# The second mixer's block compression with its operands swapped

## The reference, cut to what matters

```python
def phi(t, j):
    blocks = t[:, idx] + cmp_pos[j][None, None, :, None, :]
    flat = swapaxes(blocks, 2, 3).reshape(B, n_cmp, GROUPS, 32 * 64)
    return gelu(flat @ w1[j], approximate=False) @ w2[j]
k_cmp, v_cmp = phi(kc, 0), phi(vc, 1)         # w1[j]: 2048 x 128, w2[j]: 128 x 64
k_cmp = apply_partial_rope(k_cmp, ...)
# "cmp" attention: q . k_cmp, softmax over the 15 blocks, . v_cmp, one of three gated branches
```

## Time and profile before

| | us |
|---|---|
| median of three timed runs | 1687.31 |
| profiled execution, its own time | 1680.67 |
| its span (first to last instruction) | 1678.9 |
| mean granted TensorE clock | 0.952 of full |

### The profile page before, as it was taken

The page is one execution under the profiler, slowest core; times in us unless marked ns, Lnnn a source line. Parts: engine busy times, 40 slices in busy tenths (PEclk is TensorE's granted clock), DMA queues, the critical chain, the costliest instruction groups (busy, mean ns, idle before and its releaser), DMA issues.

```text
span 1678.9 us, 30167 instructions
## 1 busy us (share of the span) xinstructions
PE 1559.0 (93%) x10282; PEld 1427.7 (85%) x10282; DVE 1179.2 (70%) x2190; ACT 816.9 (49%) x1213; POOL 0.2 (0%) x4
## 2 busy tenths in 40 slices
PE   6899886999989999988999799799989999999997
PEld 5788775999879978976999799799978888889996
DVE  4676555788554523756458988899979999986665
ACT  6443555554455334644466566455533334334443
POOL 0000000000000000000000000000000000000000
PEclk9998989999989878979999999899989999999999
DMA  6442332565635411224557576444457777765553
GB/s 253 115 155 90 115 126 86 164 187 178 206 120 174 153 50 51 76 96 155 192 160 225 177 217 197 143 142 140 141 186 241 240 244 237 242 229 187 187 187 125
DMA packets 97772, 276.64 MB, mean 165 GB/s; under 512 B 10788, under 2 KB 37540, under 8 KB 97188
## 3 DMA queue, kind: packets, MB, share of 16 engines
q1 hardware_dynamic: 65808, 240.92, 45.1%
q10 hardware_dynamic: 31892, 34.75, 6.2%
HBM read 259.37 MB, written 16.25 MB: 164 GB/s over the span
## 4 chain that ended last, share of the span: by engine, by line
PE 82%; DVE 9%; ACT 4%; DMA 2%; issue 2%; ACTq 0%; DVEq 0%; SPq 0%; PEldq 0%
PE acc L1058 7%; PE acc L1061 7%; PE acc L1062 7%; PE ring L533 7%; PE ring L536 6%; PE ring L537 6%; PE acc L989 5%; PE acc L993 5%; PE acc L994 5%; PE acc L533 4%; PE ring L1024 3%; PE acc L537 3%; PE acc L536 3%; DVE sb_lo L1512 2%; PE ring L1045 2%
## 5 line engine op out<-in xcount | busy, mean ns | idle before, releaser
L1512 DVE TENSOR_TENSOR sb_lo<-sb_raw,sb_hi 128x1024 fp32r<-128x1024 f32 x450 | 543.8, 1223 | 220.7 <-ACT sb_hi L1120 203.3
L1120 ACT ACTIVATE sb_hi<-sb_raw 128x1024 fp32r<-128x1024 f32 x450 | 469.9, 1057 | 391.3 <-PE acc L1058 168.4
L989 PE MATMUL acc<-sb_XH,sb_hi 128*128 128x256 f32 x800 | 235.6, 295 | 18.5 <-DVE sb_lo L1512 13.3
L533 PE MATMUL ring<-sb_XH,sb_hi 128*128 128x256 f32 x784 | 224.4, 286 | 7.2 <-DVE sb_lo L1512 7.2
L993 PE MATMUL acc<-sb_XL,sb_hi 128*128 128x256 f32 x800 | 227.7, 285 | 0.0
L994 PE MATMUL acc<-sb_XH,sb_lo 128*128 128x256 f32 x800 | 227.5, 284 | 0.0
L537 PE MATMUL ring<-sb_XH,sb_lo 128*128 128x256 f32 x784 | 223.5, 285 | 0.0
L536 PE MATMUL ring<-sb_XL,sb_hi 128*128 128x256 f32 x784 | 223.4, 285 | 0.0
L1058 PE MATMUL acc<-sb_hi,sb_coefh 128*128 128x512 f32 x512 | 200.9, 392 | 7.2 <-DVE sb_coefl L2018 7.2
L1061 PE MATMUL acc<-sb_lo,sb_coefh 128*128 128x512 f32 x512 | 200.5, 392 | 0.0
L1062 PE MATMUL acc<-sb_hi,sb_coefl 128*128 128x512 f32 x512 | 200.1, 391 | 0.0
(11 more groups left out here) (315 smaller groups left out, 2631.6 us busy)
## 6 DMA issues: line engine op xcount, KB each, us to landing
sb_raw<-wstream SPq DMA_DIRECT2D x450, 512.0 KB, 3.6
ahead<-sb_early ACTq DMA_DIRECT2D x100, 128.0 KB, 2.3
sb_area<-ahead ACTq DMA_DIRECT2D x100, 128.0 KB, 3.2
sb_area<-gains ACTq DMA_DIRECT2D x4, 512.0 KB, 4.8
sb_area<-consts SPq DMA_DIRECT2D x1, 1782.0 KB, 16.4
sb_area<-mem ACTq DMA_DIRECT2D x1, 1024.0 KB, 11.5
relvec<-sb_area ACTq DMA_DIRECT2D x1, 1024.0 KB
sb_area<-keys ACTq DMA_DIRECT2D x1, 1024.0 KB, 5.2
```

The costliest lines, as they stand in the source:

```text
L533: ins = mm(out, w[0], x[0], start=first, stop=False)
L989: ins = mm(o, w[0], XH[:, c, :], start=c == 0, stop=False)
L1120: A(hi[:, r, :], raw[:, r, :], ACT.Copy).then_inc(S("hi_ready"), 1)
L1512: tt(lo[:, r, :], raw[:, r, :], hi[:, r, :].bitcast(F32), ALU.subtract).then_inc(S("lo_ready"), 1)
```

## The change

Each weight chunk of `w1[j]` is now the moving operand, with its `hi` and `lo` halves side by side (256 columns in two stretches of 128, taken from one buffer `halves` that holds both), and the 30 block columns are stationary. Each chunk takes two products, one with `kwh` and one with `kwl` stationary, 64 in all; `kwl` x `lo` is thereby computed too. The result of a j is 30 rows of two 128-wide sums (with `hi` and with `lo`), all in one bank (`crow`). ACT copies it to SBUF; four products with a 30 x 30 identity as moving operand turn it, and add the two sums, into the bank `chid` (line "chid" of the new code). `merge_half(0, 0)` stands between `crow` and the turning, `merge_half(0, 1)` between the turning and `ck2`. `crot` and `cv2` with the copies behind them move into step 0 of the attention, after `score`; only `pv` of the `cmp` units waits for `cv2_done`. On DVE the first third of `rope` now comes between `feed(cw1, 0)` and `feed(cw1, 1)`, the other two after them. On ACT both Gelus come after `feed(merge, 0)` and before `merge_copy(0)`.

```diff
@@ -167,6 +167,9 @@
         for i in range(len(units) + 2):
             if i < len(units):
                 job(("score", u0 + i), "att_scaled")
+            if units is ATT3 and i == 0:
+                job(("crot",), "crot_done")
+                job(("cv2",), "cv2_done")
             if u0 == 0 and i < len(MEM):
                 job(MEM[i], "ckv_copied")
             if 1 <= i <= len(units):
@@ -238,11 +241,9 @@
     job(("vv",), "r2_copied")
     for i in range(3):
         job(("rope", i), "roped")
-    for j in range(2):
-        job(("chid", j), "chid_done")
+    job(("crow",), "crow_copied")
+    job(("chid",), "chid_done")
     job(("ck2",), "ck2_done")
-    job(("crot",), "crot_done")
-    job(("cv2",), "cv2_done")
     attention(ATT3, len(ATT1) + len(ATT2))
     for i in range(4):
         job(("ysT", i), "ysT_ready")
@@ -291,8 +292,8 @@
         fixc = sb("fixc", at, 256)
         at += 256
         raw = sb("raw", at, NR * PC).rearrange("p (r n) -> p r n", r=NR)
-        hi = sb("hi", at + NR * PC, NR * PC, F32R).rearrange("p (r n) -> p r n", r=NR)
-        lo = sb("lo", at + 2 * NR * PC, NR * PC, F32R).rearrange("p (r n) -> p r n", r=NR)
+        halves = sb("halves", at + NR * PC, 2 * NR * PC, F32R).rearrange("p (s r n) -> p s r n", s=2, r=NR)
+        hi, lo = halves[:, 0], halves[:, 1]
         at += 3 * NR * PC
 
         XH = sb("XH", at, KC * T, F32R).rearrange("p (c t) -> p c t", c=KC)
@@ -405,6 +406,7 @@
         ofox = pl.take(NT * 512).rearrange("p (t n) -> p t n", t=NT)
         onsa = pl.take(NT * 512).rearrange("p (t n) -> p t n", t=NT)
         ott = pl.take(512)
+        crow = ott[0:2 * NCMP].rearrange("p (j s n) -> p j s n", j=2, s=2)
         mg = pl.take(NT * 2 * DM).rearrange("p (t b n) -> p t b n", t=NT, b=2)
 
         pl = Place(stage)
@@ -710,6 +712,8 @@
             def pv(u):
                 kind, t, heads, n = UNITS[u]
                 b = bank(("pv", u))
+                if kind == "cmp":
+                    pe.wait_ge(S("cv2_done"), 1)
                 pe.wait_ge(S("att_turned"), u + 1)
                 k = min(n, P)
                 nk = n // k
@@ -741,6 +745,8 @@
                         else:
                             (proj_T if MEM[i][0] == "ck" else proj_R)(MEM[i], MEM[i])
                     if units is ATT3:
+                        if i == 0:
+                            compressed_keys()
                         for j, t in merge_halves(i):
                             merge_half(j, t)
                     if 1 <= i <= len(units):
@@ -918,30 +924,42 @@
                 done(ins, ("rope", i))
 
             pe.wait_ge(S("kw_split"), 1)
+            b = bank(("crow",))[0:2 * NCMP].rearrange("p (j s n) -> p j s n", j=2, s=2)
             for j in range(2):
-                b = bank(("chid", j))
-                (q0, r0), (q1, r1_) = piece(("cw1", j), 0), piece(("cw1", j), 1)
-                for lp in range(16):
-                    k = lp % 8
-                    ins = mm3(b[:, 0:2 * NCMP], part(r0 if lp < 8 else r1_, lambda z: z[:, k * P:(k + 1) * P]),
-                              (kwh[:, j, lp, :], kwl[:, j, lp, :]), lp == 0, lp == 15,
-                              q0 if lp == 0 else q1 if lp == 8 else 0)
-                done(ins, ("chid", j))
+                for k in range(2):
+                    q, r = piece(("cw1", j), k)
+                    for i in range(8):
+                        lp = 8 * k + i
+                        rows = halves[:, :, r, i * P:(i + 1) * P]
+                        ins = mm(b[:, j], kwh[:, j, lp, :], rows, start=lp == 0, stop=False)
+                        if i == 0:
+                            ins.then_inc(S("piece_free"), 1)
+                        ins = mm(b[:, j], kwl[:, j, lp, :], rows, start=False, stop=lp == 15)
+            done(ins, ("crow",))
             pe.wait_ge(S("acc_free"), NT * 3)
             merge_half(0, 0)
-            pe.wait_ge(S("chid_done"), 2)
+            pe.wait_ge(S("crow_copied"), 1)
+            b = bank(("chid",))
+            for j in range(2):
+                for s in range(2):
+                    ins = mm(b[:, 32 * j:32 * j + 30], crow[:, j, s], ident[0:30, 0:30], start=s == 0, stop=s == 1)
+            done(ins, ("chid",))
+            merge_half(0, 1)
+            pe.wait_ge(S("chid_done"), 1)
             done(mm(bank(("ck2",))[:, 0:30], C("w2k", 0, 128), chid[:, 0, 0:30], start=True, stop=True), ("ck2",))
-            merge_half(0, 1)
-            pe.wait_ge(S("ck2_done"), 1)
-            done(mm(bank(("crot",))[:, 0:30], K("rot"), ckc[:, 0, 0:30], start=True, stop=True), ("crot",))
-            b = bank(("cv2",))
-            for g in range(2):
-                ins = mm(b[0:NCMP, g * HD:(g + 1) * HD], chid[:, 1, g * NCMP:(g + 1) * NCMP], C("w2v", 0, 64),
-                         start=True, stop=True)
-            done(ins, ("cv2",))
+
+            def compressed_keys():
+
+                pe.wait_ge(S("ck2_done"), 1)
+                done(mm(bank(("crot",))[:, 0:30], K("rot"), ckc[:, 0, 0:30], start=True, stop=True), ("crot",))
+                b = bank(("cv2",))
+                for g in range(2):
+                    ins = mm(b[0:NCMP, g * HD:(g + 1) * HD], chid[:, 1, g * NCMP:(g + 1) * NCMP], C("w2v", 0, 64),
+                             start=True, stop=True)
+                done(ins, ("cv2",))
+
             pe.wait_ge(S("fox_rows"), 1)
             pe.wait_ge(S("r2_copied"), 3)
-            pe.wait_ge(S("cv2_done"), 1)
             attention(ATT3, len(ATT1) + len(ATT2))
             pe.wait_ge(S("att_out"), len(UNITS))
             for i in range(4):
@@ -1163,6 +1181,9 @@
                             ins = A(attP[:, u % 2, k * n:(k + 1) * n], attS[:, u % 2, k * n:(k + 1) * n], ACT.Exp,
                                     bias=amx[:, u % 4, k:k + 1], accum_out=asum[:, u % 4, k:k + 1])
                         link(ins, "att_exp")
+                    if units is ATT3 and i == 0:
+                        link(A(cvr[0:NCMP].rearrange("p g d -> p (g d)"), got(act, ("cv2",))[0:NCMP, 0:P], ACT.Copy),
+                             "cv2_done")
                     if units is ATT1:
                         kind, k = name = MEM[i]
                         feed(name)
@@ -1339,14 +1360,17 @@
                 copy_job(("fv", i), fv[:, :, 256 * i:256 * i + 256], "r2_copied")
             feed(("vv",))
             copy_job(("vv",), vv, "r2_copied")
+            feed(("cw1", 0))
+            feed(("cw1", 1))
+            link(A(crow.rearrange("p j s n -> p (j s n)"), got(act, ("crow",))[0:2 * NCMP], ACT.Copy), "crow_copied")
+            feed(("merge", 0))
+            b = got(act, ("chid",))
             for j in range(2):
-                feed(("cw1", j))
-                b = got(act, ("chid", j))
-                link(A(chid[:, j, 0:30].rearrange("p (g n) -> p n g", g=2), b[:, 0:30].rearrange("p (n g) -> p n g", g=2), ACT.Gelu), "chid_done")
-            feed(("merge", 0))
+                ins = A(chid[:, j, 0:30].rearrange("p (g n) -> p n g", g=2),
+                        b[:, 32 * j:32 * j + 30].rearrange("p (n g) -> p n g", g=2), ACT.Gelu)
+            link(ins, "chid_done")
+            merge_copy(0)
             link(A(ckc[:, 0, 0:30], got(act, ("ck2",))[:, 0:30], ACT.Copy), "ck2_done")
-            link(A(cvr[0:NCMP].rearrange("p g d -> p (g d)"), got(act, ("cv2",))[0:NCMP, 0:P], ACT.Copy), "cv2_done")
-            merge_copy(0)
             attention(ATT3, len(ATT1) + len(ATT2))
             for i in range(4):
                 turned(("ysT", i), 2 * i)
@@ -1549,6 +1573,10 @@
                         else:
                             link(stt(out=o, in0=b, scalar=scale, in1=bias, op0=ALU.mult, op1=ALU.add), "att_scaled")
                         link(V.tensor_reduce(amx[:, u % 4, 0:m], o, AX.X, ALU.max, negate=True), "att_max")
+                    if units is ATT3 and i == 0:
+                        link(tt(ckc[:, 1, 0:30], got(dve, ("crot",))[:, 0:30], K("sinc"), ALU.mult), "crot_done")
+                        link(tt(ckc[:, 2, 0:30], ckc[:, 0, 0:30], K("cosc"), ALU.mult))
+                        link(tt(ckc[:, 2, 0:30], ckc[:, 2, 0:30], ckc[:, 1, 0:30], ALU.add), "cmpk_ready")
                     if units is ATT1:
                         if i < len(MEM):
                             feed(MEM[i])
@@ -1852,18 +1880,21 @@
             feed(("fv", 1))
             feed(("vv",))
             dve.wait_ge(S("ng_ready"), 1)
-            for i in range(3):
+
+            def roped(i):
+
                 b = got(dve, ("rope", i)).rearrange("p (k t) -> p k t", k=2)
                 o = t2[:, 8 + 2 * i:10 + 2 * i, :]
                 r = rt[:, i % 2, :].rearrange("p (k t) -> p k t", k=2)
                 link(tt(r, b, K("sinq").unsqueeze(1).to_broadcast([P, 2, T]), ALU.mult), "roped")
                 link(tt(o, o, K("cosq").unsqueeze(1).to_broadcast([P, 2, T]), ALU.mult))
                 link(tt(o, o, r, ALU.add), "roped_all" if i == 2 else "dve_step")
+
             feed(("cw1", 0))
```

(6 more changed lines are left out.)

## The result

| | before | after |
|---|---|---|
| median on the chip of the first comparison, us | 1687.35 (4 runs) | 1670.51 (4 runs, 1668.36 to 1671.29) |
| ratio, 95% interval | | 0.9896, 0.9878 to 0.9914 |
| profiled execution, us | 1680.67 | 1668.36 |
| its span, us | 1678.9 | 1666.5 |

Faster, as forecast, by 16.8 us between medians against 12.7 forecast, and 12.3 between the two profiled executions. The interval of this first comparison leaves out the forecast (12.7 us is a ratio of 0.9925). Two more comparisons on other chips gave 0.9922 (0.9905 to 0.9939) and 0.9925 (0.9906 to 0.9944), which both hold it: about 13 us by ratio, 15.1 and 13.1 between medians.

What follows compares the result with a forecast made beforehand. PE, busy 93% of the span, was taken as the bound. The stage's 27.5 us becoming 14.2 saves 13.3, less 0.65 coming back: 12.7 us, so 1687.31 becomes 1674.6 us, range 1669.5 to 1683.

Steps and rivals of the forecast that it cites:

- the slow clock belongs to this stage: Compression stage: 30-column products run at 1.2 GHz from 574.60, and `merge_half(0, 0)` pays part of the price.
- Layer: First compression layer on PE: 64 products of 256 moving columns at 0.1135 us each, 7.3 us.
- Turning: Added after `merge_half(0, 0)`: four fp32 products at 0.2 us each, 0.8 us, bounds 0.4 and 1.7.
- Layer to score: From the layer's first product to the first `score`: 14.2 us after the change, 27.5 before.
- The wait for `lo` before the merge half: PE before `merge_half(0, 0)`: waits 0.1 us for DVE's merge 0 pieces, at most 0.5 with the semaphores.
- `crot` and `cv2` coming back: Behind the first `score`: their 0.65 us of work returns there, while the 0.62 us wait for `cv2_done` goes.
- carrying over the 6.6 us: Whole kernel: the timed median stays 6.6 us above the profiled execution, as before the change.
- the 2 + 2 us: Allowances: 2 us each way for where the stage's clock changes, another 2 for slow clock in `score(0)` and the following merge half.
- The clock at 1.2 GHz in the new layer: Rival, chance 0.10: layer takes 13.6 us instead of 7.3, gain 3.4 us, 1683.9 us.
- the two-stretch operand at 0.213: Rival, chance 0.07: new layer's moving operand streams at 0.213 us instead of 0.1135, gain 6.3 us, 1681.0 us.
- the pace of unrounded fp32: Rival, chance 0.04: new layer's products take 0.40 us each, layer 25.6 us, 5.6 us lost, 1692.9 us.
- The given-back case: Rival, chance 0.05: attention gives back part through late chain, late merge pieces or slow clock; gain 9.6 us, 1677.7 us.

Runs made afterwards that it cites:

- DVE's order alone: Kernel before with only the first third of `rope` moved between the two feeds, old products kept: 1684.65 us, ratio 0.9999 against before.
- the swap alone: Kernel before with the new products and the turning, DVE's old order, `crot` and `cv2` ahead of the attention: 1678.94 us, ratio 0.9965.
- the change with the old order: Changed kernel with all `rope` operations on DVE put back ahead of both feeds: 1672.69 us, ratio 0.9930 against before.
- the tail alone: Kernel before with only `crot`, `cv2` and their copies moved into step 0 of the attention: 1681.67 us, ratio 0.9988.
- 32-product version: Changed kernel with `kwh` and `kwl` stationary together, six turning products, all `lo` before `rope`: 1669.78 us, 0.9912; with the change's DVE order, one execution, 1673.44 us.

## Why the prediction was right

*Mechanism.* The step "the slow clock belongs to this stage" carried most of the gain, and held: the clock falls in the old products without any idle (DVE's order alone), and the new ones keep it over a gap (the swap alone). From layer to score the granted clock was 0.67 to 0.72 in all four profiled executions with the old products. Of the ten with the new ones nine had 1.00, and the tenth, the one with 3.37 us of idle PE, 0.90. Which property of the old products does it, the 30 moving columns or the 128 stationary ones loaded for each, no run separates. Of the 12.8 us that the stage lost in the profile, the layer gives 10.4 (18.00 to 7.56), `merge_half(0, 0)` 2.2 (5.17 to 2.97) and the tail that left the stage 1.25; the turning costs 1.0. An estimate of what the clock is worth in it: j = 1 at the pace of j = 0 would have taken 48 x 0.101 = 4.8 us less, and with the 2.2 of the merge half that makes 7.0. The gap is 2.2 of the rest, and the fewer products about 3.4, less 1.0 for the turning.

*Terms.* Layer 7.3 forecast, 7.56 measured: the first step took 0.31 us, and the pace was 0.115 against 0.1135. That the two-stretch operand is the cause of this 0.0015 isn't shown, since the same stream went at 0.1165 until 570.23 and at 0.114 from there on. Merge halves 2.9 and 2.9, measured 2.97 and 2.96. Turning 0.8, measured 1.0. `ck2` 0.2, 0.23. Layer to score 14.2, measured 14.7. The wait for `lo` before the merge half, 0.1, was none. `crot` and `cv2` coming back 0.65, measured 1.0, at a granted clock of 0.57.

*What was off is the median.* 1674.6 was forecast, 1670.51 measured, inside the range. The first comparison had 16.8 us between medians, the later two 15.1 and 13.1. The step at fault is carrying over the 6.6 us by which the timed runs of before stood above its profiled one: for the change that distance was 2.2. The 4 us beyond the forecast gain in the first comparison are no merit of the prediction's mechanism: the profiles have 12.8 us in the stage (27.5 to 14.7), and the rest isn't placed. The attention behind the stage is where the profiled executions differ most. Windows from the first score to the last transpose, of before, of the change with the old order, of the tail alone:

```profile
596.50:730.10 133.60, 131.03 (x807) 114.36 (x808) 64.89 (x138) 62.39 (x176) 0.00 (x0) 0.85 0.20 64
```
```profile
584.00:719.40 135.40, 132.87 (x815) 116.15 (x814) 63.21 (x139) 62.88 (x178) 0.00 (x0) 0.85 0.18 57
```
```profile
596.10:733.30 137.20, 134.67 (x815) 117.11 (x814) 63.33 (x139) 62.91 (x177) 0.00 (x0) 0.83 0.17 55
```

With the two shown above: 133.6 us at 0.85, 137.2 at 0.83, 138.2 at 0.82, 142.7 at 0.79. PE's work is nearly the same in all, so the length follows the granted clock. Before's profiled execution has the shortest of all fourteen profiled; that it stood for a typical one was the error, and the 2 + 2 us allowed for it were few where the attention alone spans 9. The work ahead of the layer and behind the attention, the same in all versions, adds to this: the layer starts between 566.5 and 570.1, and what follows the attention spans 5 us. That before's unprofiled runs have longer attentions fits their times but isn't shown, since they leave no timeline. Whether the old products also make the attention's clock worse on average stays open too: four profiles with them give 133.6 to 142.7, the ten others 135.4 to 138.2.

*Rivals.* The clock at 1.2 GHz in the new layer, the two-stretch operand at 0.213 and the pace of unrounded fp32 are all excluded by the windows and the pace of 0.115. The given-back case happened in the profiled pair in small: 1.3 us of attention beyond the moved work.

## What to carry to other kernels

When the two operands of a product differ much in width, try the narrow one as the stationary one: the old layer loaded 128 columns of weights for each 30 that moved and took 0.112 us a product, the new one took what the moving columns cost (0.060 for 128, 0.115 for 256). Look at the granted clock beside a stream of short products: here 1.2 GHz nearly doubled the price of the second half (0.112 to 0.213 us a product) and of the unrelated merge half behind it. And before halving PE's work, follow the supply: here DVE's order decided when the `lo` pieces arrived, and so when the merge half could start. Don't take one profiled execution as the typical one where a later stage changes clock many times.

## What the runs showed of the hardware that was not expected

PE busy without a pause is no guard against 1.2 GHz: 9.40 us busy of 9.40 at 0.51, on products of 30 moving columns. An idle 2.5 us between streams of 256-column products left it at 1.00. In the 32-product version, in the one execution with 3.37 us idle, the merge half behind it began at 0.12 us a product and fell to 0.21 from 576.85 on:

```profile
576.42 0.28 PE L541 MATMUL acc<-sb_halves,sb_XH 128*128 128x256 f32 x1
...
576.85 0.42 PE L541 MATMUL acc<-sb_halves,sb_XH 128*128 128x256 f32 x1
577.07 0.42 PE L542 MATMUL acc<-sb_halves,sb_XL 128*128 128x256 f32 x1
```

Nor do 256 moving columns keep the clock by themselves. In the attention of after, behind the short products of the scores, it fell inside a merge half that had PE busy throughout (0.50 from 596.44 to 599.64):

```profile
596.16 0.28 PE L539 MATMUL acc<-sb_halves,sb_XL 128*128 128x256 f32 x1
...
596.44 0.42 PE L538 MATMUL acc<-sb_halves,sb_XH 128*128 128x256 f32 x1
596.65 0.42 PE L539 MATMUL acc<-sb_halves,sb_XL 128*128 128x256 f32 x1
```

A rounded product of 128 moving columns ran in about half the time of one of 256. The stationary operand of 60 columns in two stretches cost next to nothing over 30 in one: 32 products in 3.9 us, 0.12 each with the slow first step, where the change had 64 in 7.56.
